# Nine weight slots through the experts, and a diagonal made on ScalarE, in a two-layer trunk with 16 experts a layer

## The reference

```python
def group_moe(h, w_router, router_bias, w_gate, w_up, w_down):
    ...                      # gates: two experts of the best group per token
    def expert(y, p):
        wg, wu, wd, ge = p   # 1024x512, 1024x512, 512x1024
        a = jax.nn.silu(t @ wg) * (t @ wu) * ge[:, None].astype(t.dtype)
        return y + a @ wd, None
    y, _ = lax.scan(expert, jnp.zeros_like(t), (w_gate, w_up, w_down, gates.T))

def trunk(...):
    for i in range(DEPTH):
        ...                  # x = x + g1 * mix
        h = rmsnorm(x, norm_ffn_g[i]) * (1 + sc2) + sh2
        x = x + g2 * group_moe(h, w_router, router_bias, moe_w_gate[i], moe_w_up[i], moe_w_down[i])
    return rmsnorm(x, final_norm_g), new_k, new_v, new_sf, new_sb
```

## Time and profile before

| | us |
|---|---|
| median of three runs | 1551.95 |
| lowest and highest | 1548.06, 1553.48 |
| the profiled execution | 1553.92 |
| its span, first to last instruction | 1552.1 |
| TensorE busy | 1414.2 |
| VectorE busy | 465.0 |
| ScalarE busy | 278.9 |
| GpSimd busy | 51.4 |

### The profile page before, as it was taken

One profiled execution on the slowest core, in us unless ns is written; L12 is line 12 of the kernel. 1 busy time (PEld: TensorE's weight loads), 2 busy tenths in 40 slices (PEclk: granted clock), 3 DMA queues, 4 the chain that ended last, 5 costly groups with the idle time before them and its releaser, 6 DMA issues.

```text
span 1552.1 us, 17143 instructions
## 1 busy us (share of the span) xinstructions
PE 1414.2 (91%) x6556; PEld 724.7 (47%) x6556; DVE 465.0 (30%) x1360; ACT 278.9 (18%) x572; POOL 51.4 (3%) x71
## 2 busy tenths in 40 slices
PE   5999999989989877899999999997798998989887
PEld 2456565654444423354544544543555543444333
DVE  3056256351111124530520612504113211111254
ACT  3044245111001101120111202102101100001012
POOL 1000200000000010000000000000000100000100
PEclk9999999989999988999999999998898999999898
DMA  9878669647989996643332223334114695789961
GB/s 345 293 268 277 193 223 346 257 163 274 347 294 379 395 398 255 223 147 109 108 109 82 93 97 108 109 109 136 54 55 164 233 375 192 261 295 398 398 254 42
DMA packets 161523, 343.74 MB, mean 221 GB/s; under 512 B 5225, under 2 KB 22850, under 8 KB 161410
## 3 DMA queue, kind: packets, MB, share of 16 engines
q1 hardware_dynamic: 149744, 319.18, 56.7%
q0 software_dynamic: 2944, 9.65, 2.4%
q10 hardware_dynamic: 8722, 13.32, 2.3%
HBM read 324.96 MB, written 17.17 MB: 220 GB/s over the span
## 4 chain that ended last, share of the span: by engine, by line
PE 81%; DMA 8%; DVE 5%; ACT 2%; issue 2%; SPq 2%; DVEq 0%; ACTq 0%
PE psum L733 19%; PE psum L1025 13%; PE psum L726 11%; PE psum L1056 6%; PE psum L911 6%; PE psum L1149 5%; DMA ring<-in_moe_w_up 5%; PE psum L862 3%; PE psum L1134 3%; PE psum L628 2%; PE psum L992 2%; PE psum L963 2%; DMA ring<-in_da_w_qkv 1%; SPq L531 1%; DMA ring<-in_w_ada 1%
## 5 line engine op out<-in xcount | busy, mean ns | idle before, releaser
L733 PE MATMUL psum<-ring,hT 128*128 128x512 f32 x672 | 289.4, 592 | 0.0
L1025 PE MATMUL psum<-ring,work 128*64 128x512 f32 x480 | 224.6, 614 | 21.6 <-DMA ring<-in_moe_w_up 18.9
L1026 PE MATMUL psum<-ring,work 128*64 128x512 f32 x480 | 224.8, 614 | 0.0
L733 PEld LDWEIGHTS psum<-ring,hT 128*128 128x128 f32 x672 | 127.7, 190 | 159.0 <-issue 157.8
L726 PE MATMUL psum<-hT,ring 128*128 128x384 f32 x512 | 173.9, 498 | 8.9 <-DMA ring<-in_da_w_qkv 6.0
L1025 PEld LDWEIGHTS psum<-ring,work 128*64 128x64 f32 x480 | 64.7, 140 | 160.1 <-issue 159.6
L726 PEld LDWEIGHTS psum<-hT,ring 128*128 128x128 f32 x512 | 99.1, 195 | 78.4 <-issue 8.7
L911 PE MATMUL psum<-work 128*128 128x128 f32 x768 | 109.7, 297 | 16.0 <-issue 14.0
L1056 PE MATMUL psum<-ring,work 128*64 128x512 f32 x256 | 121.1, 617 | 0.9 <-issue 0.8
L1057 PE MATMUL psum<-ring,work 128*64 128x512 f32 x256 | 121.5, 618 | 0.0
L911 PEld LDWEIGHTS psum<-work 128*128 128x128 f32 x768 | 98.3, 205 | 38.4 <-issue 34.5
(11 more groups left out here) (306 smaller groups left out, 1469.4 us busy)
## 6 DMA issues: line engine op xcount, KB each, us to landing
ring<-in_moe_w_down SPq DMA_DIRECT2D x32, 2048.0 KB, 16.3
ring<-in_moe_w_gate SPq DMA_DIRECT2D x30, 2048.0 KB, 14.9
ring<-in_moe_w_up SPq DMA_DIRECT2D x30, 2048.0 KB, 15.6
ring<-in_w_ada SPq DMA_DIRECT2D x24, 2048.0 KB, 12.2
ring<-in_da_w_qkv SPq DMA_DIRECT2D x6, 2048.0 KB, 14.9
ring<-in_ret_w_qkv SPq DMA_DIRECT2D x8, 1024.0 KB, 8.0
ring<-in_ret_w_qkv SPq DMA_DIRECT2D x4, 2048.0 KB, 7.6
ring<-in_ret_w_gate_fwd SPq DMA_DIRECT2D x4, 2048.0 KB, 8.0
```

Of the source, the lines that this page charges most:

```text
L733: last = mm(b, hT[:, kt, P * t:P * t + P], w[:, kt, :], start=kt == 0, stop=kt == KT - 1)
L1025: mm(psum[0:BLK, x, :], xk, wg[kt], start=kt == 0, stop=kt == KT - 1)
L1026: last = mm(psum[BLK:P, x, :], xk, wu[kt], start=kt == 0, stop=kt == KT - 1)
```

## The change

In the expert stages of both layers the weights rotate through nine slots instead of six: the six of the ring and three that are made of idle tiles. Slot 6 is `sq` and a quarter unit of `yg`, slot 7 is `hT` and another, slot 8 is made of four quarters (`dg`, `ada_rows`, a part of `yg`, and `selw` with what lies behind it). The rotation covers units 0 to 35, the experts 0 to 11 (`WHOLE`); the last twelve units go through the six ring slots alone, since the spare tiles are needed by then. A load of unit 9 to 41 waits for the unit nine back, one of 42 to 47 for the unit six back. A unit in a spare slot is loaded by one DMA for each piece, so two or four. The three spare slots get semaphores like the ring's.

Since `dg` is a slot until expert 11 is done, the diagonal of the last norm can no longer be made early. ScalarE makes it now, in layer 1 at expert 12, behind a wait for twelve experts' `down`. Order and slots of retention's units are the same, counted from another place.

```diff
--- before.py
+++ after.py
@@ -54,6 +54,8 @@
     return out, number
 QC = 256
 NSLOT, SLOT = 6, 4096
+SPARES = 3
+WHOLE = 3 * LAST
 NB = 8
 LAM_INIT = 0.8 - 0.6 * math.exp(-0.3 * 0)
 BIG = 1e30
@@ -203,14 +205,30 @@
             units += [(("wo", n), ("wo", 4 * n + 3), 4 + n) for n in range(2)]
         units.append(u + (i % 4,))
     assert len(turning) % 4 == 2
-    rest = [(("moe", 0, n), None) for n in range(3 * NE - 2)]
+    order = (2, 3, 0, 1, 4, 5)
+    rest = []
+
+    def turn_in():
+
+        units.extend(u + (order[i % NSLOT],) for i, u in enumerate(rest))
+        rest.clear()
+
+    def moe(l):
+
+        wide = NSLOT + SPARES
+        for n in range(3 * NE):
+            place = n % wide if n < WHOLE else (n - WHOLE) % NSLOT
+            units.append((("moe", l, n), None, order[place] if place < NSLOT else place))
+
+    moe(0)
     for h in range(RH):
         rest += [(("rqk", h), ("rk", h, 1)), (("rv", h), ("rv", h, TT - 1)), (("rg", h, 0), ("rg", h, 0, TT - 1)),
                  (("rg", h, 1), ("rg", h, 1, TT - 1)), (("state", h), ("ro", h, TT - 1, 1))]
     rest += [(("rwo", n), ("rwo", 2 * n + 1)) for n in range(4)]
-    rest += [(("moe", 1, n), None) for n in range(3 * NE - 2)]
-    order = (2, 3, 0, 1, 4, 5)
-    return units + [u + (order[i % NSLOT],) for i, u in enumerate(rest)]
+    assert len(rest) % NSLOT == 0 and WHOLE % (NSLOT + SPARES) == 0
+    turn_in()
+    moe(1)
+    return units
 
 
 def trunk_kernel(nc, ins, outs, scratch):
@@ -237,9 +255,9 @@
     for name, who in [j for j in JOBS if j[0][0] != "yout"] + [j for j in JOBS if j[0][0] == "yout"]:
         counts[who] += 1
         evac_no[name] = (who, counts[who])
-    slot_of, full_at, prior_of, landed, latest = {}, {}, {}, [0] * NSLOT, {}
+    slot_of, full_at, prior_of, landed, latest = {}, {}, {}, [0] * (NSLOT + SPARES), {}
     for name, last_job, s in UNITS:
-        landed[s] += 16 * (2 if name[0] in ("rqk", "state") else 1)
+        landed[s] += 16 * ((2, 2, 4)[s - NSLOT] if s >= NSLOT else 2 if name[0] in ("rqk", "state") else 1)
         slot_of[name], full_at[name], prior_of[name] = s, landed[s], latest.get(s)
         latest[s] = (name, last_job)
     ada_at = {(l, u): (12 * l + u) % 2 for l in range(DEPTH) for u in range(12)}
@@ -285,10 +303,11 @@
         work = sb("work", [P, WCOLS])
 
         def carve(sizes):
-            at, out = 0, {}
+            at, out = 0, {"at": {}}
             for name, n in sizes.items():
                 assert at + n <= WCOLS, (name, at + n, WCOLS)
                 out[name] = work[:, at:at + n]
+                out["at"][name] = at
                 at += n
             return out
 
@@ -392,7 +411,10 @@
         wt_all = wm["wt"].rearrange("p (c t) -> p c t", c=2)
         shrow = wm["yg"][:, 0:2 * D].rearrange("p (c h f) -> p c h f", c=2, h=2)
         gdiag = wm["dg"].rearrange("p (k f) -> p k f", k=KT)
-        spare = [(sq, wm["yg"][:, 2 * D:3 * D]), (hT, wm["yg"][:, 0:D])]
+        flat = lambda t: t[:, :, :].rearrange("p a b -> p (a b)")
+        tail = wm["at"]["selw"]
+        spare = [[(flat(sq), 0, 3), (wm["yg"][:, 2 * D:3 * D], 3, 1)], [(flat(hT), 0, 3), (wm["yg"][:, 0:D], 3, 1)],
+                 [(wm["dg"], 0, 1), (flat(ada_rows), 1, 1), (wm["yg"][:, D:2 * D], 2, 1), (work[:, tail:tail + D], 3, 1)]]
         ytok = sq[:, :, :].rearrange("p k t -> p (k t)").rearrange("p (t d) -> p t d", t=TT)
 
         def yo(i):
@@ -407,10 +429,9 @@
         psum = ctx.enter_context(nc.psum_tensor("psum", [P, NB, 512], F))
 
 
-        spare_full = [sem(f"spare_full{i}") for i in range(2)]
         ps_filled = sem("ps_filled")
         evac = {"act": sem("act_evacuated"), "dve": sem("dve_evacuated")}
-        slot_full = [sem(f"slot_full{s}") for s in range(NSLOT)]
+        slot_full = [sem(f"slot_full{s}") for s in range(NSLOT + SPARES)]
         in_small, in_x, in_tab, in_att, in_ck, in_bc, in_wr, in_ret = (sem(n) for n in
             ("in_small", "in_x", "in_tab", "in_att", "in_ck", "in_bc", "in_wr", "in_ret"))
         pool_init = sem("pool_init")
@@ -465,9 +486,10 @@
         def bank(name):
             return psum[:, job_no[name] % NB, :]
 
-        def moe_unit(r):
-
-            return divmod(r if r < 6 else r + 2, 3)
+        def pieces(name):
+
+            s = slot_of[name]
+            return spare[s - NSLOT] if s >= NSLOT else [(ring[:, s, :], 0, 4)]
 
         def unit_wait(eng, name):
             eng.wait_ge(slot_full[slot_of[name]], full_at[name])
@@ -524,7 +546,7 @@
                         filled(sp, last_job)
                     else:
                         _, l, r = prior
-                        e, part = moe_unit(r)
+                        e, part = divmod(r, 3)
                         sp.wait_ge(M[l]["down" if part == 2 else "T"], e + 1)
                         settle(sp, l)
                 for to, src in source(name):
@@ -556,28 +578,29 @@
 
                 def expert_load(r):
 
-                    e, part = moe_unit(r)
-                    to = slot(("moe", l, r)).rearrange("p (k n) -> p k n", k=4 if part == 2 else KT)
-                    sp.dma_start(to, weights(e, part)).then_inc(slot_full[slot_of[("moe", l, r)]], 16)
-
-                def spare_load(i):
-
-                    main, rest = spare[i]
-                    by512 = lambda ap: ap.rearrange("p (k n) -> p k n", n=512)
-                    sp.dma_start(by512(main[:, :, :].rearrange("p k t -> p (k t)")), weights(2, i)[:, 0:6, :]).then_inc(spare_full[i], 16)
-                    sp.dma_start(by512(rest), weights(2, i)[:, 6:KT, :]).then_inc(spare_full[i], 16)
-
-                for k in range(6):
-                    filled(sp, prior_of[("moe", l, k)][1])
-                    expert_load(k)
+                    e, part = divmod(r, 3)
+                    name, width = ("moe", l, r), D if part == 2 else 512
+                    rows = D // width
+                    for to, at, n in pieces(name):
+                        sp.dma_start(to.rearrange("p (k n) -> p k n", n=width),
+                                     weights(e, part)[:, rows * at:rows * (at + n), :]).then_inc(slot_full[slot_of[name]], 16)
+
+                for r in range(NSLOT):
+                    filled(sp, prior_of[("moe", l, r)][1])
+                    expert_load(r)
                 filled(sp, ("rwo" if l else "wo", KT - 1))
-                spare_load(0)
+                expert_load(NSLOT)
                 filled(sp, ("htok", l, 2 * TT - 1))
                 for i in range(2 * TT):
                     emptied(sp, ("htok", l, i))
-                spare_load(1)
-                for r in range(6, 3 * NE - 2):
-                    e, part = moe_unit(r - 6)
+                expert_load(NSLOT + 1)
+                if l:
+                    sp.wait_ge(stored_s, 16 * 4 * RH)
+                else:
+                    sp.wait_ge(stored_k, 32)
+                expert_load(NSLOT + 2)
+                for r in range(NSLOT + SPARES, 3 * NE):
+                    e, part = divmod(prior_of[("moe", l, r)][0][2], 3)
                     sp.wait_ge(m["down" if part == 2 else "T"], e + 1)
                     settle(sp, l)
                     expert_load(r)
@@ -914,16 +937,9 @@
 
                 def unit(e, part):
 
-                    k = 3 * e + part
-                    if k in (6, 7):
-                        pe.wait_ge(spare_full[k - 6], 32 * (l + 1))
-                        main, rest = spare[k - 6]
-                        main = main[:, :, :].rearrange("p k t -> p (k t)")
-                        return [main[:, 512 * i:512 * i + 512] if i < 6 else rest[:, 512 * (i - 6):512 * (i - 6) + 512] for i in range(KT)]
-                    name = ("moe", l, k if k < 6 else k - 2)
+                    name, width = ("moe", l, 3 * e + part), D if part == 2 else 512
                     unit_wait(pe, name)
-                    width = D if part == 2 else 512
-                    return [slot(name)[:, width * i:width * i + width] for i in range(SLOT // width)]
+                    return [to[:, width * i:width * i + width] for to, at, n in pieces(name) for i in range(n * D // width)]
 
                 def overflow(e, wg, wu):
 
@@ -1401,6 +1417,10 @@
                                 for s in range(2):
                                     act.dma_start(scratch[e * BLK:e * BLK + BLK, 512 * s:512 * s + 512],
                                                   ysb[BLK * s:BLK * s + BLK, x, :]).then_inc(m[f"stored{x}"], 16)
+                            if l and e == LAST:
+                                act.wait_ge(m["down"], LAST)
+                                for kt in range(KT):
+                                    A(gdiag[:, kt, :], ident, ACT.Copy, scale=cols1[:, kt:kt + 1]).then_inc(gdiag_ready, 1)
                             if e == LAST + 1:
                                 act.wait_ge(m["picked"], 32 * TT)
                                 for t in range(TT):
@@ -2029,8 +2049,6 @@
```

(2 more changed lines are left out.)

## The result

The changed kernel took 1525.53 us (median of four runs, 1522.59 to 1526.26), the kernel before 1550.01 beside it (four runs, 1547.89 to 1553.48): a ratio of 0.9836, with a 95% interval of 0.9811 to 0.9862. Forecast were 1522 in a range of 1512 to 1537. The profiled execution took 1524.84 us, with a span of 1523.0; the one before had 1553.92 and 1552.1.

What follows compares the result with a forecast made beforehand. TensorE was taken to bound the kernel, losing time waiting for expert weights. From 1553.9 us profiled, 27.3 of waits and slow clock and 3 of gaps left 1523.6, as median 1522; range 1512 to 1537 for 8 in 10.

Steps and rivals of the forecast that it cites:

- The bound, and the nine slots: Experts' first products: TensorE waits for weights because loads run only two experts ahead; nine slots add up to 15.8 us lead.
- The terms: Both expert stages: waits and slow clock go, 13.9 + 3.4 us in layer 0, 7.2 + 2.8 in layer 1.
- The landing of expert 13's weights: Layer 0: expert 13's up weights land at 541 to 543 us, 14 to 16 us before they are needed.
- Expert 14: Its first loads, still waiting for expert 12's turn, and the gathered rows fit into 24.3 us, with 4 to spare.
- Rival (a): The wait moves to expert 14, 5.7 us late in each layer; 15 us given back, 1537 us; chance 0.12.
- The gaps inside the gathers: Idle time at L911, 6.0 us, from instructions late through full queues; a gain of 3 us as the queues empty.
- Rival (b): Gaps in the gathers multiply with each 100 full microseconds; 20 to 25 us given back, 1544 us; chance 0.08.
- Pieces: Spare-slot loads split into two or four DMAs, 68 loads a layer instead of 50: taken to cost nothing.
- Rival (c): Each of 18 added DMAs a layer holds the queue for 2.0 us, making the kernel slower: 1574 us; chance 0.04.
- The diagonal: ScalarE in layer 1 behind expert 12's copies: 2.5 us of work under 13 us of idle time, cost 0.
- The numbers: Whole kernel: profiled execution 1523.6 us, median 2 us below it, said as 1522, own range 1513 to 1533.

Runs made afterwards that it cites:

- e6: The nine-slot kernel without the loads of units 9 to 47 in both layers, computing from whatever the slots hold: 1506.07 us, ratio 0.9706.
- e12: The nine-slot kernel without every expert's overflow block and its branch, on all engines: 1470.21 us, ratio 0.9457.
- e7: The nine-slot kernel with 128 more instructions at the head of TensorE's program: 1524.67 us, ratio 0.9831.
- e9: The nine-slot kernel with 256 more instructions at the head of TensorE's program: 1546.57 us, ratio 0.9973.
- e5: The nine-slot kernel with every expert unit of the ring loaded by four DMAs of 512 KB instead of one: 1520.54 us, ratio 0.981.
- e4: The kernel before, with only the last norm's diagonal moved from GpSimd to ScalarE: 1551.41 us, ratio 1.0008.

## Why the prediction was right, point by point

**The bound, and the nine slots.** Right. The waits for loads are gone in both layers, they come back with six slots, and they go by the slot.

**The terms.** Layer 0: 13.9 + 3.4 = 17.3 us forecast, 17.3 measured as the stage's change. That the two agree to a tenth is luck: from expert 9's start to expert 14's the stage is 18.8 us shorter, and 1.5 us were lost before expert 9. Layer 1: 7.2 + 2.8 = 10.0; from expert 12's start to expert 14's 10.5 were won, and 11.4 in the whole stage. The profiled execution fell by 29.1 us against 27.3 of the sum; by the medians it is 24.5. The two medians differ less than the two profiled executions because those lay at opposite sides of theirs: the one before 3.9 us above its four runs' median, the one after 0.7 below.

**The landing of expert 13's weights.** The step was mis-sized: 541 to 543 us was forecast, and it was 550.36. Two things are missing in it. Unit 27 went out at 467.63, not 465.3, since expert 6 itself starts 2.3 us later (447.58 against 445.28); the queues had run empty before that, even with nine slots, as the sum assumes. And fourteen units are not all that moves. The windows and the queues of the changed kernel, from 462 and in 467 to 551 us, show both:

```profile
462.00:467.00 5.00, 4.30 (x52) 3.22 (x52) 1.31 (x5) 0.00 (x0) 0.00 (x0) 1.00 0.10 35
```

```profile
q1 hardware_dynamic: 12858, 30.45, 95.7%
q10 hardware_dynamic: 1107, 1.67, 5.4%
q8 instruction: 9, 0.15, 0.7%
```

The first moves 35 GB/s for five microseconds. In the second 30.45 MB are weights (fourteen units are 29.4), and 1.67 MB are the experts' results on their way to HBM, which the sum left out: 4.2 us at 397 GB/s. So 467.6 + 14 x 5.27 + 4.2 + 3.4 = 549.0, against 550.36. The lead of 14 to 16 us was one of 8.8; the forecast needed only that it be above zero.

**Expert 14.** Room of 4 us was forecast and 7.5 measured. Rival (a) is dead in both layers: no wait for a load at all. The up load took 20.9 us from issue to landing (555.12 to 576.00), not the 30.0 that the rival borrowed.

**The gaps inside the gathers.** This step failed, though the change was faster all the same. A gain of 3 us was taken because the queues would be near empty when experts 12 and 13 gather. They moved 375 GB/s there: the gathered rows and expert 14's weights took the place of the late loads. The gaps are 9.0 us in four, where they were 8.5. Their cause was named half: instructions late in full queues is what e6 and the packets show, but the jump over the block is the other half (e12), and the place decides which products are hit (e7, e9). Rival (b) would have needed more gaps with more full microseconds; the number of long gaps in the gathers stayed at three in layer 0 and two in layer 1.

**Pieces.** Taken as nothing, and nothing it was (e5). The 2.0 us a DMA of the page, taken in series, are not seen in the stream. Rival (c) is dead.

**The diagonal.** 2.5 us under 13 of cover forecast; 2.44 us with 10.52 of idle time behind them (so 13.0 in all), and e4 shows no effect.

**The numbers.** For the profiled execution 1523.6 were forecast, and it took 1524.84. The 3 us of the gathers didn't come and the first stretch took 0.9 more, while layer 1's stage gave 1.4 more and the stretch between the stages 1.3, neither of which was forecast: part of the small miss of 1.2 us is luck. The median was set 2 us below the profiled execution, as before, and came out 0.7 above it: 1522 against 1525.5. The forecast's own range, 1513 to 1533, doesn't follow from its terms: 5 us of more gain and 9 + 4 of less around 1522 are 1517 to 1535.

## What to carry to other kernels

Where weights stream through slots, count how many microseconds of stream the slots hold, and look for windows in which the queues idle while the consumer will later wait; more lead moves those idle microseconds to where they are needed, and two slots of 5.27 us each took away all but 1.3 us of waits of up to 9.3 us here. Count all that shares the queues in a landing sum: results stored, rows gathered, the program's own blocks. If an engine shows idle time that nothing releases in the midst of equal instructions, look for a packet of the instruction queue in the gap, shift the program by half a block and then by a whole one, and look for a jump.
